# First layer norm split over ScalarE, VectorE and GpSimd, with its scale and shift at the PSUM copies

## The reference, cut to what matters

```python
h = layer_norm(ALPHA * h + mix(h), ln1_g, ln1_b)      # ALPHA = 2 ** 0.25
ff = moe_ffn(h, w_router, router_bias, w_gate, w_up, w_down, ws_gate, ws_up, ws_down)
h = layer_norm(ALPHA * h + ff, ln2_g, ln2_b)

def layer_norm(x, g, b):
    mu = mean(x); var = mean((x - mu) ** 2)
    return (x - mu) * rsqrt(var + EPS) * g + b
```

## Time and profile before

| | us |
|---|---|
| Median of 3 runs (2271.69 to 2273.22) | 2273.07 |
| Span of the profiled execution | 2272.0 |
| TensorE busy | 2222.8 (98%) |
| VectorE busy | 1159.8 (51%) |
| ScalarE busy | 692.0 (30%) |
| GpSimd busy | 13.0 (1%) |
| Mean DMA rate | 280 GB/s |

### The profile page before, as it was taken

One profiled execution on the slowest core, in us unless ns is written; L12 is line 12 of the kernel. 1 busy time (PEld: TensorE's weight loads), 2 busy tenths in 40 slices (PEclk: granted clock), 3 DMA queues, 4 the chain that ended last, 5 costly groups with the idle time before them and its releaser, 6 DMA issues.

```text
span 2272.0 us, 32579 instructions
## 1 busy us (share of the span) xinstructions
PE 2222.8 (98%) x12776; PEld 1608.6 (71%) x12776; DVE 1159.8 (51%) x1461; ACT 692.0 (30%) x761; POOL 13.0 (1%) x28
## 2 busy tenths in 40 slices
PE   8999999999999999999999999999999999999996
PEld 8999999999988888888887954444444444444442
DVE  5356666666665554555456734444444443344335
ACT  4333433434344334334334411111111111111112
POOL 1000000000000000000000000000000000000000
PEclk9999999999999999999999999999999999999998
DMA  7444434444445555555658289999999999999996
GB/s 282 139 168 141 166 130 149 158 149 141 149 166 190 199 185 197 191 187 194 228 193 299 109 375 428 426 428 428 429 428 429 429 429 428 428 428 429 428 428 279
DMA packets 62183, 635.45 MB, mean 280 GB/s; under 512 B 7424, under 2 KB 7552, under 8 KB 10384
## 3 DMA queue, kind: packets, MB, share of 16 engines
q1 hardware_dynamic: 60192, 627.30, 70.3%
q0 software_dynamic: 752, 4.75, 0.6%
q10 hardware_dynamic: 1152, 2.10, 0.2%
HBM read 632.02 MB, written 2.10 MB: 279 GB/s over the span
## 4 chain that ended last, share of the span: by engine, by line
PE 73%; DMA 18%; DVE 5%; ACT 2%; issue 2%; SPq 0%; DVEq 0%; ACTq 0%
PE bank L304 25%; PE bank L272 19%; DMA wgu<-wgu 16%; PE bank L852 13%; PE bank L900 5%; PE bank L527 3%; PE bank L800 3%; PE bank L810 3%; DVE wlo L1222 1%; DMA raw<-units 1%; ACT whi L948 1%; DVE wlo L1559 1%; DVE cv L1337 1%; DMA wdt_raw<-wdt 1%; PE bank L833 0%
## 5 line engine op out<-in xcount | busy, mean ns | idle before, releaser
L1222 DVE TENSOR_TENSOR wlo<-raw,whi 128x2048 fp32r<-128x2048 f32 x185 | 424.0, 2292 | 397.9 <-ACT whi L948 395.8
L948 ACT ACTIVATE whi<-raw 128x2048 fp32r<-128x2048 f32 x185 | 353.9, 1913 | 430.1 <-PE bank L304 320.0
L852 PE MATMUL bank<-wgu,xg 128*64 128x512 f32 x2048 | 448.8, 593 | 4.1 <-DMA wgu<-wgu 4.1
L852 PEld LDWEIGHTS bank<-wgu,xg 128*64 128x64 f32 x2048 | 145.6, 137 | 300.4 <-issue 281.9
L272 PE MATMUL bank<-xhi,whi 128*128 128x256 f32 x896 | 260.5, 291 | 3.9 <-DVE wlo L1222 3.9
L272 PE MATMUL bank<-xhi,wlo 128*128 128x256 f32 x896 | 253.4, 283 | 0.0
L272 PE MATMUL bank<-xlo,whi 128*128 128x256 f32 x896 | 253.4, 283 | 0.0
L900 PE MATMUL bank<-wd,eactT 128*64 128x512 f32 x1024 | 226.8, 595 | 0.0
L304 PE MATMUL bank<-whi,xhi 128*128 128x512 f32 x512 | 199.8, 390 | 0.0
L1739 DVE SCALAR_TENSOR_TENSOR eact<-eth,bank 128x256 f32<-128x256 f32 x32 | 13.5, 422 | 364.7 <-issue 192.7
L304 PE MATMUL bank<-whi,xlo 128*128 128x512 f32 x512 | 199.2, 389 | 0.0
(11 more groups left out here) (364 smaller groups left out, 3409.3 us busy)
## 6 DMA issues: line engine op xcount, KB each, us to landing
wgu<-wgu SPq DMA_DIRECT2D x128, 2048.0 KB, 21.6
raw<-units SPq DMA_DIRECT2D x204, 1024.0 KB, 5.0
wd<-wd SPq DMA_DIRECT2D x64, 2048.0 KB, 18.7
raw<-units SPq DMA_DIRECT2D x6, 512.0 KB, 6.9
stage<-units SPq DMA_DIRECT2D x2, 1024.0 KB, 12.9
h<-xtok POOLq DMA_DIRECT2D x2, 1024.0 KB, 8.6
out<-acc SPq DMA_DIRECT2D x3, 512.0 KB, 2.6
stage<-units SPq DMA_DIRECT2D x2, 512.0 KB, 9.2
```

Source lines behind the costliest of these rows:

```text
L852: mi = nc.tensor.matmul(bank[3][CAP * j:CAP * j + CAP, :], buf[:, 4 * c + k, CAP * (2 * half + j):CAP * (2 * half + j + 1)], wgu_t[c][:, j ...
L948: nc.scalar.activation(whi[u % SPLIT][:, :], raw[u % RAW][:, :], ACT.Copy).then_inc(hi_done, 1)
L1222: V.tensor_tensor(wlo[u % SPLIT][:, :], raw[u % RAW][:, :], whi[u % SPLIT][:, :].bitcast(f32), ALU.subtract).then_inc(lo_done, 1)
```

## The change

The normalised rows z = (h - mean)/sd are now made without gain and bias, and stay in `htok`: half 0 by ScalarE (Identity with a scale and a bias operand of one value for each token), half 1 by VectorE (one TENSOR_SCALAR per chunk). Gain and bias are then applied at three places:

- on the transposed side at the copy from PSUM to `hT`, where they are one value per partition (new tile `lncol`, loaded early), in two instructions of 256 elements for each bank; the cast to `hhi` moves from ScalarE to VectorE;
- on the gathered tokens at the copy to `xg`, in the same way, on ScalarE and VectorE, in all pairs. The gathering matmuls and `h_tok_hi`, `h_tok_lo` now carry z;
- on the residual: GpSimd makes `acc = z * gain + bias` in two instructions for each half. ALPHA is applied when the down matmuls are added (`acc * ALPHA + bank`).

`lng[0]` and `lnb[0]` move to the place of `wlo`, so their loads wait for the end of the output units. The statistics of half 0 are finished before half 1's are begun. Unread matmuls: 2 and 6.

```diff
+    lncol = at("ln1_columns", 95.5, [P, 2, KT])
@@ gpsimd
+        pool.wait_ge(unit_used, N_S0 - N_X)
         pool.dma_start(lng[0][:, :], lnp[0].partition_broadcast(P)).then_inc(og["ln_in"], 16)
         pool.dma_start(lnb[0][:, :], lnp[1].partition_broadcast(P)).then_inc(og["ln_in"], 16)
+        pool.wait_ge(og["ln_in"], 32)
+        for t in range(TT):
+            pool.wait_ge(og[("z0_ok", "z1_ok")[t]], 4)
+            nc.gpsimd.tensor_tensor(acc[t][:, :], htok[:, t, :], lng[0][:, :], ALU.mult)\
+                .then_inc(og["scaled_ok"], 1)
+            pool.wait_ge(og["scaled_ok"], t + 1)
+            nc.gpsimd.tensor_tensor(acc[t][:, :], acc[t][:, :], lnb[0][:, :], ALU.add)\
+                .then_inc(tk["acc_ok"], 1)
@@ tensor
-        keep_running(26)
-        turns(0)
-        turns(1)
+        keep_running(2)
+        turns(0, 0)
+        turns(1, 0)
+        keep_running(6)
+        turns(0, 1)
+        turns(1, 1)
+        turns(2, 0)
+        turns(2, 1)
         logits(0)
+        turns(3, 0)
+        turns(3, 1)
         pe.wait_ge(og["res_ok"], 8 + START)
         shared(0)
-        turns(2)
-        turns(3)
@@ scalar
+        norm_root(0)
+        act.wait_ge(og["stats_ok"], 2)
+        for c in range(4):
+            z = htok[:, 0, c * 512:(c + 1) * 512]
+            nc.scalar.activation(z, z, ACT.Identity, bias=bnr[:, 0, 3:4], scale=bnr[:, 0, 2:3]).then_inc(og["z0_ok"], 1)
+        norm_root(1)
+        def columns(out, b, k, j):
+            return nc.scalar.activation(out[:, k, :], b[:, j * S:(j + 1) * S], ACT.Identity, bias=lncol[:, 1, k:k + 1],
+                                        scale=lncol[:, 0, k:k + 1])
         for k2 in range(KT // 2):
             act.wait_ge(og["tr_ps"], k2 + 1)
-            nc.scalar.activation(hT[:, 2 * k2:2 * k2 + 2, :], b, ACT.Copy).then_inc(og["ht_ok"], 1)
-            nc.scalar.activation(hhi[:, 2 * k2:2 * k2 + 2, :], b, ACT.Copy).then_inc(og["hi_ok"], 1)
+            columns(hT, bank[3 + k2 % 4], 2 * k2, 0)
+            columns(hT, bank[3 + k2 % 4], 2 * k2 + 1, 1).then_inc(og["ht_ok"], 1)
-        nc.scalar.activation(acc[0][:, :], htok[:, 0, :], ACT.Copy, scale=ALPHA).then_inc(tk["alpha_ok"], 1)
-        nc.scalar.activation(acc[1][:, :], htok[:, 1, :], ACT.Copy, scale=ALPHA).then_inc(tk["alpha_ok"], 1)
@@ vector
+        norm_stats(0)
+        norm_root(0)
+        norm_stats(1)
+        norm_root(1)
+        for c in range(4):
+            z = htok[:, 1, c * 512:(c + 1) * 512]
+            V.tensor_scalar(z, z, bnr[:, 1, 2:3], bnr[:, 1, 3:4], ALU.mult, ALU.add).then_inc(og["z1_ok"], 1)
+        def h_high(k2):
+            V.tensor_copy(hhi[:, sl, :], hT[:, sl, :]).then_inc(og["hi_ok"], 1)
-        token_low(0)
@@ vector, gathered: the copies to xg
-            V.tensor_copy(xg[buf][:, 2 * i:2 * i + 2, :], bank[b][:, :].rearrange("p (k s) -> p k s", k=2))\
-                .then_inc(ex["xg_dve"], 1)
+            for j2 in range(2):
+                k = 2 * i + j2
+                ins = V.tensor_scalar(xg[buf][:, k, :], bank[b][:, j2 * S:(j2 + 1) * S], lncol[:, 0, k:k + 1],
+                                      lncol[:, 1, k:k + 1], ALU.mult, ALU.add)
+            ins.then_inc(ex["xg_dve"], 1)
@@ vector, behind the router
+        token_low(0)
         token_low(1)
@@ vector, the sum of the down matmuls
-            V.tensor_tensor(acc[t][:, sl], acc[t][:, sl], bank[SH_BANK[i % 5]][:, :], ALU.add).then_inc(sh["acc_ok"], 1)
+            V.scalar_tensor_tensor(acc[t][:, sl], acc[t][:, sl], ALPHA, bank[SH_BANK[i % 5]][:, :], ALU.mult, ALU.add)\
+                .then_inc(sh["acc_ok"], 1)
```

More of the change, by code:

```diff
@@ L73, with build_trunk @@
 Q4 = 4 * CAP
-def build_trunk(nc, units, params, hnorm, wdt, dtb, alog, poolm, poolw, xtok, lnp, wrt, rbias, wgu, wd, out):
+def build_trunk(nc, units, params, hnorm, wdt, dtb, alog, poolm, poolw, xtok, lnp, lnc, wrt, rbias, wgu, wd, out):
     base = 16512
@@ L723, in keep_running, with turns @@
                 nc.tensor.matmul(bank[7][:, :], s_hi[0][:, 0:P], s_hi[0][:, 0:512], start=True, stop=True)
-        def turns(c):
+        def turns(c, t):
             if c >= 2:
[L728 to L739, removed]
+                pe.wait_ge(og["ht_ok"], 2 * c - 2)
+            pe.wait_ge(og[("z0_ok", "z1_ok")[t]], c + 1)
+            for k2 in (2 * c, 2 * c + 1):
+                for j in range(2):
+                    k = 2 * k2 + j
+                    mi = nc.tensor.transpose(bank[3 + k2 % 4][:, j * S + t * P:j * S + (t + 1) * P],
+                                             htok[:, t, k * P:(k + 1) * P], ident[:, :])
+                if t == TT - 1:
+                    mi.then_inc(og["tr_ps"], 1)
         def logits(c):
-            pe.wait_ge(og["w_in"], 32)
+            pe.wait_ge(og["w_in"], 48)
             pe.wait_ge(og["ht_ok"], 2 * c + 2)
@@ L1154, in gathered @@
             act.wait_ge(ex["ga_ps"], blocks + j + 1 + START)
-            nc.scalar.activation(xg[buf][:, 2 * i:2 * i + 2, :], bank[b][:, :].rearrange("p (k s) -> p k s", k=2),
-                                 ACT.Copy).then_inc(ex["xg_act"], 1)
+            columns(xg[buf], bank[b], 2 * i, 0)
+            columns(xg[buf], bank[b], 2 * i + 1, 1).then_inc(ex["xg_act"], 1)
         def first_gathered(j):
@@ L1570, in chunk_stats @@
                 lstep(V.bn_stats(bns[:, t, c, :], src[t][:, c * 512:(c + 1) * 512]))
-        def norm_stats(k):
-            for t in range(TT):
-                lstep(V.bn_aggr(bna[:, t, :], bns[:, t, :, :]))
-            V.tensor_scalar(bnr[:, :, 0:1], bna[:, :, 1:2], EPS, None, ALU.add).then_inc(og["stats_ok"], 1)
-            dve.wait_ge(og["sd_ok"], k + 1)
-            lstep(V.reciprocal(bnr[:, :, 2:3], bnr[:, :, 1:2]))
-        def norm_scale(k, t, sl):
-            v = (htok[:, t, :], acc[t])[k][:, sl]
-            lstep(V.scalar_tensor_tensor(v, v, bna[:, t, 0:1], lng[k][:, sl], ALU.subtract, ALU.mult))
-            V.scalar_tensor_tensor(v, v, bnr[:, t, 2:3], lnb[k][:, sl], ALU.mult, ALU.add).then_inc(og["scaled_ok"], 1)
         for what, j in LAST[5:-2]:
@@ L1594, in _, with norm_stats @@
                 chunk_stats([htok[:, t, :] for t in range(TT)], c)
-        dve.wait_ge(og["half_ok"], 1)
-        for t in range(TT):
+        def norm_stats(t):
             residual(3, 16 * t, (t,))
```

81 lines of the change are left out of this document (45 added, 36 removed).

## The result

| | us |
|---|---|
| Kernel before, median of 9 runs (2270.53 to 2273.87) | 2271.69 |
| Changed kernel, median of 9 runs (2275.54 to 2279.66) | 2278.59 |
| Ratio, 95% interval | 1.0026 [1.0017, 1.0034] |
| Forecast (range 2269.0 to 2282.5) | 2277.4 |

The change costs 6.9 us, where the prediction's sum had 4.3; the time itself is met within 1.2 us, partly because the kernel before came out 1.4 us lower here than in the three runs that the forecast was built on. Taken again beside the last experiments, the same kernel gave 2277.95 (8 runs), ratio 1.0024 [1.0014, 1.0035].

A forecast was written before the change was run, and what follows sets the result against it. The prediction took the pairs as DMA-bound and VectorE's chain as setting the down matmuls' start. Router +1.1, token_low(0) +2.2 and gather copies +1.0 gave +4.3: span 2276.3, forecast 2277.4 us, range 2269 to 2282.5.

The forecast's parts named there:

- What bounds the kernel: Expert pairs are DMA-bound at 428 GB/s; moving the start of the down matmuls moves the end one for one.
- Statistics to logits: Half 0 goes ahead in the norm: shared(0) starts 2.4 us sooner, the last logits end 4.1 us sooner.
- Blocking in turn: Before the router, one VectorE instruction runs between two of GpSimd's, 4.0 us each: selection +1.1 us; chance 0.42.
- TensorE is no limit: Under blocking, TensorE waits for chunk 2's hlo until 1288.2 and has shared(2) done at 1294, without limiting.
- Rival D: TensorE's clock falls while thinly busy from 1260.5 to 1269.8: +0.8 us under blocking, 2274.6 without; chance 0.06.
- token_low(0) and the gather copies: token_low(0) moves behind the router, +2.2 us; two-piece gather copies before the down matmuls, +1.0 us (0.3 to 1.3).
- A: No GpSimd blocking that matters, router from 1281.4: -2.5 us, 2270.6; chance 0.20.
- B: VectorE goes first, GpSimd gets no turn until 1273.8, router caught only in part: 2273.3 us; chance 0.14.
- C: GpSimd clearly slower, 5.2 us an instruction, holding up hhi and hlo work: +9.1 us, 2282.2; chance 0.14.
- E: An expert pair becomes longer than the DMA's 29.4 us: +3 to +10 us; chance 0.04.
- the forecast's own case: GpSimd and VectorE block in turn, GpSimd instruction 3.6 to 4.6 us: 2275 to 2280 us; chance 0.42.

The follow-up runs named there:

- gpsimd_after_split: Changed kernel with GpSimd's four residual instructions held back until the last hlo is made: 2274.44 us, ratio 1.0009 to the kernel before.
- more_unread: Changed kernel with 20 more unread matmuls between the last logits and shared(1): 2277.70 us, ratio 1.0030 to the kernel before.
- acc_on_vectore: Changed kernel with GpSimd's four residual instructions moved to VectorE behind the last subtraction: 2269.66 us, ratio 0.9992 to the kernel before.
- h_by_tokens_on_vectore: Changed kernel with the four instructions on VectorE, h_tok_hi and h_tok_lo taken from acc, plain gather copies: 2267.16 us (0.9980), again 2268.59 (0.9986).

## Why the prediction was right, and where its sizes were off

**What bounds the kernel.** Right. The end moves with the down matmuls one for one, in 14 of 14 traces.

**Statistics to logits.** Right. Counted from the last output matmul, `shared(0)` starts at 10.3 us against 12.4 (1264.92 and 1272.05; forecast -2.4, measured -2.1), and the last logits end at 21.6 against 25.4 (forecast -4.1, measured -3.8). None of it is worth anything here, because VectorE is not ready.

**Blocking in turn.** The mechanism is right, and shown three ways: taken out (8 to 9 us less), put into the old kernel (9 more), cut small (4 to 5 less). Two sizes in it were off, in opposite directions. The instruction was put at 4.0 us, from the waiting copy, and is 4.58. With VectorE's turn in between, four took 19.4 us in place of 17.5. The 4497 ns of the Trainium skill (GPSIMD Engine Reference, Performance versus the Vector engine) is nearer to the measured length than my reading was. And it began sooner: 8.1 us after the last output matmul and not 10.3, since the loads of gain and bias landed sooner: 7.3 us after the first was issued, where the prediction has 9.3 (and its own terms, with the issue of 0.5, add up to 9.8). The ends nearly cancel (27.5 against a forecast 27.8). But the earlier start caught more of VectorE's work: seven casts and subtractions were left behind GpSimd's end and not four, and the router started at 31.4, against 29.0 before and a forecast of 30.1: **+2.4 where I had +1.1**. There is luck in the total: by the prediction's own price, 0.4 for each 0.1 us of a GpSimd instruction, 4.58 us alone would give 4.3 + 2.3 = 6.6, close to the 6.5 measured. But the earlier start took 1.0 of it off again (the router +2.4 and not 1.1 + 2.3 = 3.4), and the wait for the ranks, which that sum does not have, put 0.95 on.

**"TensorE is no limit."** This sentence failed. I had it waiting for the third chunk's `hlo` until 1288.2 and done with `shared(2)` at 1294, which is 34 us after the last output matmul. It waited already for the second chunk's, idled 6.5 us, worked at half clock, and ended `shared(2)` at 1296.4 in the trace after, 42 us after that matmul and 1.1 behind the router's selection (1295.24). VectorE then waited 1.04 us for the ranks; before it had no such wait. That is the missing **+0.95**. By these rows it is the clock's share: `shared(1)` and `shared(2)` took 13.78 us, and at twice 5.81 they would have ended ahead of the selection. Rival D's price (0.8 under blocking) agrees with it by chance: it was worked out for a clock lost through the few unread matmuls, and this one was lost through the blocking.

**token_low(0) and the gather copies.** +2.2 as forecast, and +0.9 where I had +1.0. The sum of the terms with their measured sizes is 2.4 + 0.95 + 2.2 + 0.9 = 6.45 us, the stage's difference; the forecast had 4.3.

**The rivals.** A and B (no blocking, VectorE first) are out by the rows of VectorE. B had a true part: MAX8 is not caught. C's size (5.2 us) was not reached, but 4.58 is past the 4.1 us from which the prediction let C decide, and the loss is past its 4.5: the result lies between the forecast's own case and C. E did not occur: the rest is constant.

By the Trainium skill (SBUF — State Buffer, Who interferes with whom) the lock holds for the whole instruction, for two-input work and for VectorE's fast copies. The traces agree: a cast of one source was held for 4.4 us (4.82 less 0.42, changed kernel), an addition of two for 3.4 (3.64 less 0.29, gpsimd_after_split). The rows of before had shown it for two-input work only.

## What to carry to other kernels

Work given to GpSimd while VectorE is on the critical path is paid by VectorE: each of its instructions that reads two tensors, casts, or is a TENSOR_SCALAR (the router's first took 0.96 and 1.32 us in place of 0.22) waits for the GpSimd instruction then running, so the cost is the number of VectorE's instructions caught times the length of one of GpSimd's. Before moving element-wise work to GpSimd, look whether VectorE has a wait for something else that it fits into; here 9.1 us of it fitted into such a wait, and the ranks were read at the same 34.36 us with it and without it. If it must be GpSimd, cut it into short instructions and lay it beside reductions such as MAX8, and measure stages from a common event, since the length ahead of them differed by 5 us between the traces of before and after. Before a difference of 1 us between two traces is put down to an edit, compare the granted clock in the same stretch.

## What the runs showed that was not expected

- RECIPROCAL (0.95) and MAX8 (3.23 for 16) keep their length beside GpSimd, while an addition of 128x128 takes 3.64 and not 0.29.
- GpSimd's TENSOR_TENSOR of 128x2048 takes 4.58 us with two different tensors, and 3.60 with one tensor as both operands (3.93 with its wait).
- The granted clock fell to 0.50 after an idle time of 6.5 us, but to 0.64 (mean of 4 us) also after one of 2.0 us behind a busy stretch (more_unread), and to 0.50 after waits of 1.6 to 1.7 us in the first gathers (acc_on_vectore, h_by_tokens_on_vectore) and once in a stretch where TensorE worked 2.6 of 4 us. Other traces have the last two stretches with the clock at 1.00 throughout.
